# The opening of a two-block token-mixing kernel: norm before the first weight split, statistics per token block, first product by pairs

## What is computed

```python
def rmsnorm(x, w):
    xf = x.astype(jnp.float32)
    y = xf * lax.rsqrt(jnp.mean(xf * xf, axis=-1, keepdims=True) + EPS)
    return (y * w.astype(jnp.float32)).astype(x.dtype)
...
        h = rmsnorm(x, norm_mix[l])
        proj = h @ w_in[l]
        a_q, a_f, a_i, a_g, b_x, b_g, c_q, c_k, c_v, c_g, c_lr = jnp.split(proj, IN_SPLITS, axis=-1)
```

## Time and profile before

| | before |
|---|---|
| median of 3 runs | 1544.21 us |
| the profiled execution | 1546.39 us |
| its span | 1545.1 us |
| PE busy | 1427.2 us, 92% |
| PEld busy | 1302.2 us, 84% |
| DVE busy | 866.6 us, 56% |
| ACT busy | 681.0 us, 44% |
| POOL busy | 97.1 us, 6% |
| DMA | 230.79 MB, mean 149 GB/s |

### The profile page before, as it was taken

The page is one execution under the profiler, slowest core; times in us unless marked ns, Lnnn a source line. Parts: engine busy times, 40 slices in busy tenths (PEclk is TensorE's granted clock), DMA queues, the critical chain, the costliest instruction groups (busy, mean ns, idle before and its releaser), DMA issues.

```text
span 1545.1 us, 23177 instructions
## 1 busy us (share of the span) xinstructions
PE 1427.2 (92%) x9749; PEld 1302.2 (84%) x9750; DVE 866.6 (56%) x1175; ACT 681.0 (44%) x982; POOL 97.1 (6%) x138
## 2 busy tenths in 40 slices
PE   4899799999999998898899999999998898999997
PEld 4788799988899998766889999899988756889997
DVE  4687656657545464454754456545564454655555
ACT  4456344544434443445344443444433444344432
POOL 1133000000000000250000000000000250000000
PEclk9898889999999999968999999999999767999999
DMA  5333266766565653500565566665653500465651
GB/s 164 108 108 123 82 204 191 225 182 191 165 201 180 186 169 97 183 1 1 146 197 185 180 182 183 189 194 173 183 162 110 171 0 1 137 210 172 191 183 64
DMA packets 294672, 230.79 MB, mean 149 GB/s; under 512 B 10139, under 2 KB 277290, under 8 KB 294314
## 3 DMA queue, kind: packets, MB, share of 16 engines
q1 hardware_dynamic: 294554, 229.31, 48.6%
q10 hardware_dynamic: 16, 0.00, 0.0%
HBM read 228.24 MB, written 1.05 MB: 148 GB/s over the span
## 4 chain that ended last, share of the span: by engine, by line
PE 77%; DVE 13%; ACT 6%; DMA 2%; issue 2%; SPq 0%; DVEq 0%; ACTq 0%
PE bank L726 22%; PE bank L727 22%; PE bank L728 22%; PE bank L1073 3%; DVE lo_gu L1497 3%; PE bank L1103 3%; ACT hi_gu L1152 2%; PE bank L1090 1%; PE bank L736 1%; PE bank L1034 1%; PE bank L928 1%; DMA st_gu<-in_ffn_w_gu 1%; DMA st_gu<-in_ffn_w_val 1%; DVE stats L1524 1%; PE bank L938 1%
## 5 line engine op out<-in xcount | busy, mean ns | idle before, releaser
L726 PE MATMUL bank<-xTh,hi_gu 128*128 128x256 f32 x1736 | 495.6, 285 | 8.3 <-DVE big L1701 5.8
L727 PE MATMUL bank<-xTl,hi_gu 128*128 128x256 f32 x1736 | 494.8, 285 | 0.0
L728 PE MATMUL bank<-xTh,lo_gu 128*128 128x256 f32 x1736 | 494.7, 285 | 0.0
L1497 DVE TENSOR_TENSOR lo_gu<-st_gu,hi_gu 128x2048 fp32r<-128x2048 f32 (+1 forms) x140 | 317.4, 2268 | 224.4 <-ACT hi_gu L1152 224.4
L726 PEld LDWEIGHTS bank<-xTh,hi_gu 128*128 128x128 f32 x1736 | 337.0, 194 | 11.6 <-issue 7.2
L727 PEld LDWEIGHTS bank<-xTl,hi_gu 128*128 128x128 f32 x1736 | 336.9, 194 | 1.7
L728 PEld LDWEIGHTS bank<-xTh,lo_gu 128*128 128x128 f32 x1736 | 336.8, 194 | 0.0
L1152 ACT ACTIVATE hi_gu<-st_gu 128x2048 fp32r<-128x2048 f32 (+2 forms) x145 | 273.0, 1883 | 39.8 <-DMA st_gu<-in_ffn_w_gu 19.1
L726 PE MATMUL bank<-hi_dn,actTh 128*128 128x512 f32 x436 | 171.7, 394 | 10.8 <-DVE actTl L1630 7.4
L726 PE MATMUL bank<-hi_gu,xTh 128*128 128x256 f32 (+1 forms) x576 | 168.6, 293 | 13.9 <-DVE xTl L1512 9.4
L727 PE MATMUL bank<-lo_dn,actTh 128*128 128x512 f32 x436 | 170.3, 391 | 0.0
(11 more groups left out here) (262 smaller groups left out, 1536.8 us busy)
## 6 DMA issues: line engine op xcount, KB each, us to landing
st_gu<-in_ffn_w_gu SPq DMA_DIRECT2D x176, 512.0 KB, 5.1
st_dn<-in_ffn_w_down SPq DMA_DIRECT2D x109, 512.0 KB, 6.4
st_gu<-in_w_in SPq DMA_DIRECT2D x27, 1024.0 KB, 5.5
st_gu<-in_w_out SPq DMA_DIRECT2D x12, 1024.0 KB, 5.2
st_gu<-in_ffn_w_gate SPq DMA_DIRECT2D x21, 512.0 KB, 5.1
st_gu<-in_ffn_w_val SPq DMA_DIRECT2D x21, 512.0 KB, 6.4
gb<-in_ln_g SPq DMA_DIRECT2D x6, 512.0 KB, 7.0
gb<-in_ln_b SPq DMA_DIRECT2D x6, 512.0 KB, 8.1
```

The source lines that it names most:

```text
L726: pe.matmul(o, lhs[0], rhs[0], start=start, stop=False, **kw)
L727: pe.matmul(o, lhs[0], rhs[1], start=False, stop=False, **kw)
L728: return pe.matmul(o, lhs[1], rhs[0], start=False, stop=stop, **kw)
L1497: dve.tensor_tensor(split_view(low_of(c), c), split_view(st_gu[c % 2], c), split_view(high_of(c), c).bitcast(F32), ALU.subtract).then_inc( ...
```

## The change

The semaphore of x is split in two, one for each token block. VectorE begins with block 0 as soon as it is there, and does the first half of block 1's statistics between block 0's variance and its reciprocal. ScalarE loads the Sqrt table first, does the scaling of both blocks, copies the gain columns in between, and only then makes the high part of chunk 0, ahead of the high parts of h. GpSimd clears its buffers first and makes chunk 0's low part last. The first product waits for h pair by pair instead of for the last pair. SP's instructions are the same and in the same order; what its wait for the cleared gate buffers waits for comes earlier in GpSimd's program.

```diff
-        x_loaded, ident_loaded = signal("x_loaded"), signal("identity_loaded")
+        x_loaded, ident_loaded = [signal(f"x_loaded{m}") for m in range(M)], signal("identity_loaded")
...
-                sp.dma_start(x[:, m, :], A["x"][0, m * P:(m + 1) * P, :]).then_inc(x_loaded.sem, x_loaded.dma(m))
+                sp.dma_start(x[:, m, :], A["x"][0, m * P:(m + 1) * P, :]).then_inc(x_loaded[m].sem, x_loaded[m].dma(0))
...
-            weights_low(0)
             for g in range(2):
                 pool.memset(wab[g], 0.0).then_inc(cleared_p.sem, cleared_p.one("gates" if g == 1 else None))
             pool.memset(zeros[:, :], 0.0).then_inc(cleared_p.sem, cleared_p.one("zeros"))
             pool.memset(xpv, 0.0).then_inc(cleared_p.sem, cleared_p.one("xp"))
+            weights_low(0)
...
-            def t_block(c, z, b):
+            def t_block(c, z, b, first=False):
 
                 wait_low(pe, c)
                 for k in range(KD):
+                    if first and k % 2 == 0:
+                        pe.wait_ge(h_low.sem, h_low[0, k // 2])
...
-            pe.wait_ge(h_low.sem, h_low[0, 3])
-            t_block(0, 0, 4)
+
+            t_block(0, 0, 4, first=True)
...
             def first_norm():
                 for m in range(M):
+                    act.wait_ge(x_loaded[m].sem, x_loaded[m][0])
                     act.wait_ge(var_done.sem, var_done[0, m])
...
+                    if m == 0:
+                        act.wait_ge(first_cols_turned.sem, first_cols_turned[0])
+                        act.activation(par1[:, 0:8], bank[0][:, 0:8], ACT.Copy).then_inc(first_cols_ok.sem, first_cols_ok.one(0))
+                weights_high(0)
+                act.wait_ge(first_cols_ok.sem, first_cols_ok[0])
                 for j in range(KD // 2):
...
-            weights_high(0)
-            act.wait_ge(first_cols_turned.sem, first_cols_turned[0])
-            act.activation(par1[:, 0:8], bank[0][:, 0:8], ACT.Copy).then_inc(first_cols_ok.sem, first_cols_ok.one(0))
             act.preload_act_table(ACT.Sqrt)
-            act.wait_ge(x_loaded.sem, x_loaded[1])
-            act.wait_ge(first_cols_ok.sem, first_cols_ok[0])
             first_norm()
...
+                dve.wait_ge(x_loaded[0].sem, x_loaded[0][0])
                 statistics(0, 0, 0)
                 statistics(0, 0, 1)
                 variance(0, 0)
+                dve.wait_ge(x_loaded[1].sem, x_loaded[1][0])
+                statistics(0, 1, 0)
                 scales(0)
-                statistics(0, 1, 0)
                 statistics(0, 1, 1)
...
-            dve.wait_ge(x_loaded.sem, x_loaded[1])
             first_norm()
```

## The result

The changed kernel takes 1534.97 us (median of six runs, 1534.32 to 1536.1), the one before 1544.63 (six runs, 1543.34 to 1546.69): ratio 0.9936, 95% interval 0.9924 to 0.9949. It is 9.7 us faster; forecast were 7.9 (1536.3, within 1534.0 to 1540.5).

A forecast was written before the change was run, and what follows sets the result against it. TensorE takes 77% of the span, so only the serial opening before its first product could gain. Moving that start from 24.51 to 16.60 us saves 7.9: 1544.2 - 7.9 = 1536.3 us, range 1534.0 to 1540.5.

The forecast's parts named there:

- Start of the product: TensorE's first product, behind GpSimd's split of chunk 0: from 24.51 to 16.60 us, 7.9 us gained.
- ScalarE's way to the high part: ScalarE's table load, roots, copies and scaling summed end to end; free for chunk 0's high part at 10.08 us.
- The 0.4 us booked for the half in front of the reciprocal: VectorE does half of block 1's statistics first, so block 0's reciprocal comes at 7.17, not 6.75: cost 0.4 us.
- I take no delay: VectorE's low parts of h beside GpSimd's split are not held, because they read PSUM: 0 us added.
- rival B: VectorE held by GpSimd during the low parts of h: product starts at 17.5, time 1537.2 us; chance 0.10.
- The PSUM row: Profile row: four tensor_tensor with one PSUM input, 1.68 us, ran straight through a 2.63 us GpSimd operation.
- Rival C: Chunk 0 lands late through the moved DMAs: product starts between 16.6 and 23.65, 1536.3 to 1543.3 us; chance 0.12.
- Chunk 2: Load issued at 16.6, wanted at 24.2: lands at 22.0, or 1.4 us late against 1.3 slack; costs 0 to 0.1.
- rival D: Gain given back in the first section, chunk 2 behind the moved loads: 1537.1 us, up to 1542; chance 0.09.
- Clock: First 3.4 us of the product at 1.2 GHz, then 2.4; each half-speed us loses 0.41 us.
- The allowance of 1.4 us "if there were none": No half-speed stretch at all at the product's start would add 1.4 us to the gain.
- Rival E: Longer idle time leaves TensorE at 1.2 GHz through the seven blocks: 4.5 us slower, 1548.7 us; chance 0.04.

The follow-up runs named there:

- stats_in_order: Changed kernel with the first half of block 1's statistics put back behind block 0's reciprocal; 1536.19 us in a single run.
- undo_pool: Changed kernel with GpSimd again making chunk 0's low part first and its four memsets after it; 1548.44 us, kernel before 1545.23, ratio 1.0020.
- undo_pool_queue: undo_pool with SP also issuing chunk 2's load before its wait for the cleared gate buffers; 1536.4 us, kernel before 1545.3, ratio 0.9937.
- changed_again: The changed kernel, unedited, measured and profiled again beside halves_again; 1535.98 us, kernel before 1545.3, ratio 0.9942.
- halves: Changed kernel with chunk 0's high and low parts each in two instructions, first product waiting for the half it reads; 1533.02 us, before 1544.3, ratio 0.9936.
- halves_again: The same program as halves, measured once more in the rounds of changed_again; 1532.58 us, kernel before 1545.3, ratio 0.9924.
- only_pool: Kernel before with only GpSimd's four memsets moved ahead of its split; 1542.0 us, kernel before 1545.23, ratio 0.9979.
- fill_gap: Changed kernel with five unused matmuls of zeros between TensorE's transposes and the first product; 1534.93 us, kernel before 1544.3, ratio 0.9940.
- undo_pairs: Changed kernel with the first product waiting for the last pair of h again; 1535.11 us, kernel before 1545.23, ratio 0.9932.

## Why the prediction was right

**Start of the product.** Forecast 16.60, found 16.21 and 16.16. The order of events is as forecast: ScalarE free about when chunk 0 lands, GpSimd's split last, h ready before it. The mis-sized term is ScalarE's way to the high part, 9.66 instead of 10.08: the second root came 0.3 earlier, at 8.61 and not 8.90, since ScalarE's neighbouring instructions overlap (the copy of the gain columns starts at 8.55, before the copies of block 0 end at 8.64), where the sum had put end to start. The eight high parts of h took 3.01 us and not 3.40: in the kernel before they followed the transposes pair by pair, the last of which ended at 22.67, and here they begin 1.8 us behind the first transpose and not 1.1, and don't have to wait for the later ones.

**The 0.4 us booked for the half in front of the reciprocal** is the step that was wrong, on its sign: stats_in_order loses 0.5 us by putting it back, because ScalarE's second root then waits for block 1's variance.

**Contention.** "I take no delay" holds: 3.23 us beside GpSimd, and rival B is out. The PSUM row was the right neighbour.

**Rival C** did not happen, but it was hardly put to the test. The prediction had the 1.8 MB issued while chunk 0 was still on its way; SP needs 0.4 to 0.8 us for each issue, and only 0.26 MB of them were out when chunk 0 landed at 9.2. In undo_pool, without them, it took 8.2 us and not 7.1. The rule of the Trainium skill that a ring's descriptors are taken in order ("DMA: Bandwidth & Descriptors", section "Queues, rings and completion order") is not contradicted by that. Chunk 2 took 5.4 to 7.4 us where it was issued ahead of or well behind the 1.8 MB, and 9.0 to 10.3 right behind them. But order alone doesn't give these figures: in undo_pool_queue chunk 3, issued at 22.6 right behind the same 1.8 MB, took 6.0 us, and in undo_pool chunk 3, issued 0.5 us behind chunk 2, landed within 0.5 us of it. What sets a landing there stays open.

**Chunk 2** was seen as the thing that doesn't move with the work, and forecast right at no cost, so rival D is out: TensorE is busy all through from 18 to 38 us. But the prediction never asked what the order of the memsets is worth; it booked them as cover on VectorE alone. It is worth 13 us, more than the whole gain: without it the other edits make a slower kernel. The price of a late chunk was also short. It is the wait and the half-speed restart together: in undo_pool 6.5 us of idle time cost 9.2 between the end of block (0,1) and the end of the block run (25.65 to 49.24, against 32.09 to 46.49 before). Another 1.2 us went ahead of that, in the longer slow stretch at the product's start.

**Clock.** In its first profile the changed kernel has a slow stretch of 3.4 us like the one before (3.6), only it begins 0.9 us into the product. That this term came out as forecast is luck: in changed_again the stretch is 5.3 us, in halves nothing and in halves_again 1.9, and over all profiles it runs from nothing to 6.1 us (undo_pool). So the number of slow matmuls does change between runs of one kernel, which the prediction could not yet see. The allowance of 1.4 us "if there were none" is what only_pool and fill_gap show in the blocks. Rival E, half speed through all seven blocks, did not happen.

**What is left.** The gain in the medians is 9.7 us and not 7.9. Of the 1.8 between them 0.4 is the start of the product, and 0.4 is that the prediction subtracted from 1544.2, the median of three runs, where that of six is 1544.6. The remaining 1.0 may lie in the half-speed stretches further on, which the prediction left at their old length; no run shows that it does.

## What to carry to other kernels

When a consumer is made to start earlier, look for the load it will want next and see what that load's queue waits for: here the order of GpSimd's split and its memsets, which SP waits for, stood between 10 us gained and 3 us lost. A split that the first product waits for is worth cutting into pieces that follow the product's own order, but only together with waits of the same grain. A long stall on TensorE (6.5 us here) costs its length and then the restart at half speed. And one profile of the changed kernel is not enough to say how long TensorE is slow: take a second before explaining a microsecond by it.

## What was not expected of the hardware

The transposes alone can bring TensorE to full speed: in halves the engine does nothing but float32 transposes from 9.29 to 13.5, the last small one still in 0.40 us, and the product behind them runs at 0.12 us a matmul from the second one; in undo_pairs that last transpose (84x84) already takes 0.29. When it happens differs between executions of one program: halves_again has eight matmuls at 0.21 behind the same transposes. After 2.3 us of idle time (changed kernel) six matmuls ran at 0.12 and then one in 0.21 until 20.5; in changed_again, after 2.5 us, all were slow from the first. In the kernel before, 1.25 us of idle time behind the same transposes were followed by 3.6 us at 0.21, in only_pool 1.35 us by none. So the length of the gap doesn't decide it alone; what else does, these profiles don't show.
